# All forty projection blocks beside HGRN's levels as two-part products, with the low parts made by GpSimd

## The reference

```python
def hybrid_mixer(xn, w_in, lb, ...):
    proj = jnp.einsum('bld,dc->blc', xn, w_in)
    q, zf_fwd, zf_bwd, inp, og, hy, gates = jnp.split(proj, IN_SPLITS, axis=-1)
    ...
    logf_f, k_f = forget(zf_fwd)          # log(lb + (1 - lb) sigmoid(z)), (1 - lb) sigmoid(-z)
    logf_b, k_b = forget(zf_bwd)
    qh, vh = jax.nn.silu(heads(q, HGRN_DK)), heads(inp, HGRN_DV)
    o2 = hgrn2_chunk_scan(...)            # both directions: S_t = diag(f_t) S_{t-1} + k_t v_t^T, o_t = S_t^T q_t
    o = rmsnorm(o2[:B] + rev(o2[B:]), hgrn_norm_g).reshape(B, L, HGRN_WIDTH)
    y_a = jnp.einsum('blc,cd->bld', o * jax.nn.silu(og), w_branch_a)
    ...
    g_a, g_b = jnp.split(gates, N_BRANCHES, axis=-1)
    merged = jax.nn.sigmoid(g_a) * y_a + jax.nn.sigmoid(g_b) * y_b
```

## The kernel before

| turn | levels of the pair | fetched / multiplied after it, third pair |
|---|---|---|
| 0 | DVE: four partings each (L2423 to L2430), differences of SBUF tiles | w30 / w28 |
| 1 | ACT: two Exps each (L2465, L2467) | w31 / w29 |
| 2 | DVE: three multiplications each (L2434, L2437, L2438) | w56 / w30 |
| 3 | PE: first half of the scores (L2487) | w57 / w31 |
| 4 | PE: second half; DVE: copies of the first half (L2453, L2454, L2456) | w58 / w56 |
| 5 | DVE: copies of the second half | w59 / w57 |

## Time and profile before

### The profile page before, as it was taken

One profiled execution on the slowest core, in us unless ns is written; L12 is line 12 of the kernel. 1 busy time (PEld: TensorE's weight loads), 2 busy tenths in 40 slices (PEclk: granted clock), 3 DMA queues, 4 the chain that ended last, 5 costly groups with the idle time before them and its releaser, 6 DMA issues.

```text
span 2527.7 us, 39068 instructions
## 1 busy us (share of the span) xinstructions
PE 2372.7 (94%) x15354; PEld 2141.8 (85%) x15354; DVE 1658.8 (66%) x3195; ACT 1342.3 (53%) x2494; POOL 770.8 (30%) x404
## 2 busy tenths in 40 slices
PE   6878998999999999998888888999999999999998
PEld 5876888999999888887867876789999999888886
DVE  4564457967777566665657475666977788566665
ACT  3344444468888444444533454244458888444443
POOL 3000002877776000000700053101887777000000
PEclk8888899999999999999999998999999999999999
DMA  5322334555555566664332343245555555566663
GB/s 175 122 94 70 94 99 153 176 177 165 165 163 170 179 192 193 190 191 140 117 122 87 125 135 109 67 150 159 184 176 162 165 162 163 184 192 192 191 193 123
DMA packets 108286, 383.36 MB, mean 152 GB/s; under 512 B 12975, under 2 KB 15840, under 8 KB 107528
## 3 DMA queue, kind: packets, MB, share of 16 engines
q1 hardware_dynamic: 108104, 380.86, 48.4%
HBM read 379.74 MB, written 1.06 MB: 151 GB/s over the span
## 4 chain that ended last, share of the span: by engine, by line
PE 81%; DVE 11%; ACT 4%; DMA 2%; issue 2%; POOL 0%; SPq 0%; DVEq 0%; ACTq 0%; POOLq 0%
PE psum L370 23%; PE psum L372 22%; PE psum L371 22%; PE psum L2042 2%; PE psum L402 2%; DVE weight_parts L343 2%; ACT weight_parts L338 1%; PE psum L616 1%; PE psum L2707 1%; PE psum L2487 1%; PE psum L1468 1%; PE psum L1029 1%; PE psum L1369 0%; PE psum L1199 0%; PE psum L1791 0%
## 5 line engine op out<-in xcount | busy, mean ns | idle before, releaser
L349 POOL TENSOR_TENSOR weight_parts<-weight_ring,weight_parts 128x1024 fp32r<-128x1024 f32 x276 | 670.5, 2440 | 505.7 <-ACT weight_parts L338 505.3
L370 PE MATMUL psum<-acts_high,weight_parts 128*128 128x256 f32 x2744 | 793.8, 289 | 22.4 <-DVE weight_parts L343 10.5
L372 PE MATMUL psum<-acts_high,weight_parts 128*128 128x256 f32 x2744 | 782.2, 285 | 0.0
L371 PE MATMUL psum<-acts_low,weight_parts 128*128 128x256 f32 x2744 | 781.8, 285 | 0.0
L338 ACT ACTIVATE weight_parts<-weight_ring 128x1024 fp32r<-128x1024 f32 x674 | 709.8, 1054 | 128.4 <-PE psum L372 60.7
L343 DVE TENSOR_TENSOR weight_parts<-weight_ring,weight_parts 128x1024 fp32r<-128x1024 f32 x398 | 487.6, 1226 | 306.6 <-ACT weight_parts L338 306.5
L370 PEld LDWEIGHTS psum<-acts_high,weight_parts 128*128 128x128 f32 x2744 | 531.6, 194 | 33.7 <-issue 12.5
L371 PEld LDWEIGHTS psum<-acts_low,weight_parts 128*128 128x128 f32 x2744 | 532.1, 194 | 1.3 <-issue 0.5
L372 PEld LDWEIGHTS psum<-acts_high,weight_parts 128*128 128x128 f32 x2744 | 532.0, 194 | 0.0
L370 PE MATMUL psum<-weight_parts,peer_coef 128*128 128x512 f32 x1024 | 404.0, 394 | 4.0 <-issue 3.9
L371 PE MATMUL psum<-weight_parts,peer_coef 128*128 128x512 f32 x1024 | 401.7, 392 | 0.0
(11 more groups left out here) (426 smaller groups left out, 3137.5 us busy)
## 6 DMA issues: line engine op xcount, KB each, us to landing
weight_ring<-in_peer_down SPq DMA_DIRECT2D x128, 512.0 KB, 3.6
weight_ring<-in_peer_up SPq DMA_DIRECT2D x128, 512.0 KB, 4.2
weight_ring<-in_peer_u SPq DMA_DIRECT2D x128, 512.0 KB, 3.6
weight_ring<-in_peer_v SPq DMA_DIRECT2D x128, 512.0 KB, 3.6
weight_ring<-in_w_in SPq DMA_DIRECT2D x88, 512.0 KB, 3.6
weight_ring<-in_w_out SPq DMA_DIRECT2D x16, 512.0 KB, 3.6
weight_ring<-in_peer_w_q SPq DMA_DIRECT2D x16, 512.0 KB, 4.1
weight_ring<-in_w_in_v SPq DMA_DIRECT2D x10, 512.0 KB, 3.5
```

The source lines that it names most:

```text
L349: q.e.tensor_tensor(self.low, self.ring, self.high.bitcast(F32), ALU.subtract).then_inc(*self.unit.ready.once())
L370: q.e.matmul(out, sh, mh, start=first, stop=False)
L371: q.e.matmul(out, sh, ml, start=False, stop=False)
L372: return q.e.matmul(out, sl, mh, start=False, stop=last)
```

## The change

No unit of the forty is fetched whole any more. `c.whole` is never set, `in_turns` goes, and `c.low_by` is set to "pool" as soon as the forget gates' blocks are planned, ahead of the flush that fetches q's first two blocks, and not only in `finish`. Since `work` is no longer read by products, what the heads wait for before they write into it is the last product.

```diff
             late_channels(c, [w[8 + n] for n in range(2 * KD)], gained, make_keys, make_norm)
-            c.whole = True
+            c.low_by = "pool"
             c.flush(w[0], w[1])
...
-            def in_turns(units):
-
-                for n, _ in enumerate(units):
-                    c.whole = n < 14 or n % 2 == 0
-                    yield
-
             gates = []
-            filler = in_turns(more())
+            filler = more()
 
             def finish():
                 for _ in filler:
                     pass
-                c.whole = False
-                c.low_by = "pool"
                 c.flush(w[32], w[40])
-                return xn.whole_free
+                return c.last_product
```

## The result

The changed kernel takes 2563.18 us (median of 4 runs, 2556.46 to 2572.35), the kernel before 2531.63 us beside it (4 runs, 2528.5 to 2533.27): a ratio of 1.0134, with a 95% interval of 1.0113 to 1.0155. It is 31.5 us slower. The profiled span went from 2527.7 to 2556.5 us.

The account below looks back on a forecast made before the run. PE was taken to bound q and the tail, a circular chain through DVE, ACT and PE the pairs. 10 + 2.7 + 18.8 - 2 = 29.5 us on the 2527.7 span gives 2557.2; with 4.4 for the median, 2562 us, range 2537 to 2582.

Parts of the forecast that it names:

- q, +10: q's eight blocks: low parts on POOL delay the second Ln and block 2, so q ends 10 us later (+6 to +14).
- v, +2.7: Units of v: the third's rounding waits behind four Exps, its product precedes the first scores; 2.7 us more (0 to +5 on top).
- The pairs, +18.8: Pairs of levels: shorter waits gain, five low parts colliding with DVE lose; 5.4 + 6.9 + 6.5 us (-15 to +25).
- The price, 2.16 us: Pairs of levels: each POOL low part colliding with a two-input DVE instruction costs DVE 2.16 us, five a pair, 10.8.
- TensorE's clock: Sign in the profile: PE's clock would be lower in the pairs; no size given.
- The tail, -2: After the levels: five whole blocks save 0.55 us each, two roundings behind gate activations cost 0.8; -2 us (-4 to +1).
- the 0.55: On PE: a block in parts takes 2.9 us against 3.45 whole, 0.55 saved, counting only where PE sets the pace.
- The 4.4 us between span and median: Whole kernel: the timed median of 2532.15 us lay 4.4 above the profiled span of 2527.7, an offset used for the forecast.
- DVE's busy time in a pair: Sign in the pairs of levels: DVE's busy time up by some 8 to 10 us while PE's falls.
- no collisions: Rival for the pairs: low parts fall into DVE's idle gaps, pairs gain 15 us; -8.3 in all, 2524 us; chance 0.08.
- POOL waiting DVE's run out: Rival for the pairs: low parts wait for back-to-back DVE instructions to end, DVE loses little; +5, 2537 us; chance 0.08.
- the argument from L2751: In the spectrum, POOL's L2751 ended before DVE's L2756 had run, taken as evidence against POOL waiting out DVE's whole run.

Follow-up runs that it names:

- the run without reads: The changed kernel, but GpSimd makes each of the forty low parts by a memset of zeros, reading no SBUF: 2521.85 us, 0.9967 of the kernel before.
- the all-whole one: The kernel before, but all forty blocks multiplied whole, with nothing rounded or subtracted for them: 2533.71 us, 1.0001 of the kernel before.
- the kernel with VectorE's first two low parts: The changed kernel, but VectorE makes the low parts of q's first two blocks: 2559.63 us, 1.0114 of the kernel before; one repeat gave 2564.24 us.
- the one with a single read: The changed kernel, but each low part is GpSimd's product of the raw block with zero, one SBUF tensor read: 2534.49 us, 1.0016 of the kernel before.

## Why the prediction was right

2562 us was predicted with a range of 2537 to 2582, and 2563.18 measured. The four terms hold one by one, each within its bounds; in the pairs some of the closeness is luck.

- **q, +10: +9.7.** The second Ln came at 1263.60 (forecast 1265.3, in a stretch that began 1.4 us earlier), block 2 reached PE at 1269.02 (1271) after 5.81 us idle (5), its matmuls ran at the lower clock to about 1274.3, and q's last Keep was at 1288.88. The granted clock is 0.57 from 1252.6 to 1260.4, 0.70 from 1262.9 to 1274.2 with the idle time in it, and 1.00 behind that (the second of these windows is below). What I had not written down is the first of them: block 0, too, is late, by 2.98 us, ahead of the longer wait. That queues and not turns are the larger part the run without reads shows (7.0 of 9.7 stay). GpSimd's two low parts ahead of the last keys, with their turns, are 5.4 of it; the other 4.3 stay when VectorE makes these, with block 2's rounding behind both Ln on ACT.

```profile
1262.93:1274.20 11.27, 5.46 (x27) 5.26 (x26) 9.38 (x6) 5.29 (x6) 8.30 (x4) 0.70 0.28 83
```

- **v, +2.7: +3.3.** The low part of the third unit does stand behind four Exps and its product ahead of the scores: 1304.79 on PE (forecast 1306.5).
- **The pairs, +18.8: +20.9.** The two sides were measured apart. Gain, by the run without reads against before: 3.0, 4.9 and 4.9, 12.8 in all; the forecast had 4.3, 5.4 and, for a fourth pair of 33.4 that comes to 29.5, 3.9: 13.6. Loss: 33.7; the forecast had three times 10.8, 32.4. In the third and the fourth pair five of six low parts collide and the sixth is free, as ACT's queue said, but in the second only four collide. The price, 2.16 us from two instructions of the spectrum, was that of the levels (3.38 less 1.22). So fourteen collisions and not fifteen make 30.2 us. That the loss still came to 33.7, close to the forecast, is luck: 3.5 us of it stand in no term. A part of these is TensorE's clock, which the prediction names as a sign but does not price here. The first scores of the second level took 3.75 us in each of these pairs (in the third from 1392.41, after 5.21 us idle); in the run without reads they took 2.02, 2.45 and 2.02. The rest is not resolved.
- **The tail, -2: -3.9**, at the favourable bound, of which 1.0 is the mark: in the kernel before the last Keep stood behind a rounding on ACT that waited for its load (below). On PE, from the fourth pair's second-half scores to the heads' first matmul, the tail went from 37.05 us (1409.57 to 1446.62) to 34.15 (1442.11 to 1476.26). That is 2.9, five blocks at 0.58, so the 0.55 was right and the two roundings behind the gates' activations cost nothing of the 0.8 that I gave them. In the table only the kernel before and the all-whole one have this 1.0, so the sums of the others against before are as much too favourable.

```profile
1446.87 1.06 ACT L338 ACTIVATE weight_parts<-weight_ring 128x1024 fp32r<-128x1024 f32 x1 [1.50 <-DMA weight_ring<-in_w_in]
1447.83 0.37 ACT L546 ACTIVATE gate_b<-psum 128x256 f32<-128x256 f32 x1
```

The 4.4 us between span and median was 6.7 this time (2563.18 less 2556.5). Of the signs two came out a little otherwise: DVE's busy time in a pair rose by 7.5 us and not by 8 to 10, and PE's did not fall but stayed at 28.6. Of the rivals, "no collisions" is what the run without reads measures (-7.4 against the -8.3 worked out). POOL waiting DVE's run out was not wrong in kind: it does occur, in the kernel with VectorE's first two low parts and in the one with a single read, where the argument from L2751 would have excluded it.

## What to carry to other kernels

Before moving work to an idle GpSimd, look at whether it reads SBUF and what VectorE does in that stretch: 2.4 us of GpSimd subtraction cost 2.2 us of VectorE's chain in fourteen places out of seventeen, more than the 1.23 it took on VectorE. The same work was free where VectorE copied out of PSUM or idled, so that the border belongs right behind VectorE's last run, and it has to be set with the prefetch in mind: free buffers let the first such instruction run ahead into it (36.4 against 30.8 us for that pair, with 29 and 31 blocks whole). And a faster product is worth little where what it needs lengthens the chain of another engine. The three pairs took 94.6 us with whole blocks, 87.3 with blocks in parts whose low parts read nothing, and 120.9 with GpSimd's subtractions; 31 blocks whole and nine in parts take 0.9961 of the time of the mix before, where all in parts take 1.0134.

## What the runs showed of the hardware

- A GpSimd read that meets a run of VectorE instructions either gets in at the next boundary or waits for the whole run. In the kernel after the low part at 1379.86 got in 0.29 us after it started; in the kernel with VectorE's first two low parts the one at 1297.88, with the same 0.29 us to the boundary and before the same line, L2438, took 8.17 us and came only behind the run. What decides was not found.
- With one tensor read by GpSimd VectorE waited 0.85 us of the read's 2.77, and then both went on together. The Trainium skill (SBUF — State Buffer, "Who interferes with whom") says that the pair of ports that the two engines share is an exclusive lock: whoever issues first has it for the whole instruction, and the other is blocked. For the subtraction, which reads two tensors, the trace agrees (2.15 us of about 2.4); for the single read the measurement is lower.
- VectorE's scans are also held: eight took 13.32 us and not 4.74 beside four low parts. A copy from SBUF to SBUF (L2423), 0.69 before, took 2.83 beside one, and 2.01 beside memsets that read nothing; so the rule as the prediction quotes it, that an instruction with at most one SBUF input is not held, is too wide. The Trainium skill (SBUF — State Buffer, "Who interferes with whom") excepts VectorE's two-port modes from it; no run here shows the mode of this copy. The copies out of PSUM through a mask did not change (1.32).
